# A first norm summed from rows of x, the norm of group A in other steps, and products of the identity beside the transposes

## The chip, the cores and the metric

The kernel runs on one core of one Trainium2 chip, as one launch. The time is the device time in microseconds (us). Matrix products run on TensorE (PE), whose operands come from SBUF and whose sums go to PSUM; VectorE (DVE), ScalarE (ACT) and GpSimd (POOL) do the rest. SyncE (SP) and ACT issue the transfers from memory. The engines run side by side, each through its own queue in order, and wait for each other on semaphores.

## What is computed

Two transformer blocks over one sequence of 512 tokens of width 1024, in float32. The change touches the first block alone:

```python
h = rms_norm(x, norm_mix_pre)            # mean of x*x over the 1024 columns of a token
proj = h @ w_in                          # 1024 -> 1536
qa, ka, va, qb, kb, vb = split(proj)     # 8 heads of 64 and 2 key heads, twice
qa = rope(rms_norm(qa, q_norm_a)); ka = rope(rms_norm(ka, k_norm_a))
out_a = global_attention(qa, ka, va)
out_b = window_attention(rope(qb), rope(kb), vb, sink_b)
mixed = concat(rms_norm(out_a, group_norm_a), rms_norm(out_b, group_norm_b)) @ w_out
x = x + rms_norm(mixed, norm_mix_post)
# a gated feed-forward follows, and a second block with other mixers
```

## The kernel before

**Products.** Activations lie with features on the 128 partitions and the 512 tokens along the row. Each wide product is made as three: weight and activation are split into a high and a low part (`w_hi`, `w_lo`, `h_hi`, `h_lo`), and `three` (L492) sums hi*hi, hi*lo and lo*hi in one PSUM bank. Weights come in units of 1 MB in three slots: SP loads a unit to `w_raw` (`load`, L420), `split` makes the high part on ACT (L981) and the low part on DVE (L433). A chunk is 128 output columns: 8 input tiles, so 24 products of 128x512.

**Start.** `in1` is the product with w_in, in chunks j = 0 to 11; chunks 9 to 11 are made during attention. Chunks 0 and 1 are made together (`first_units`, L516), tile after tile, as the eight tiles of x and the four quarters of unit 0 land: ACT makes `h_hi` (L1030) and the quarters' high parts, DVE the low parts (L1514 to L1520). h leaves out the norm's factor, a number per token, which goes in later. Its sum of squares: ACT squares each tile of x, POOL adds them up in `sqsum` (L462), and PE sums `sqsum` and the last square over the partitions with `ones` (`total`, L547, eight products). Then DVE has the variance, ACT the first guess of the root (`guess`, L996), DVE refines it (`factors`, L1461), and PE turns it along the rows (`factor`, L589). `beside` (L662) places this small work on PE behind the chunks: `total` behind chunk 2, `factor` behind chunk 3; `item` (L600) transposes V or sums the squares of a normed head over its 64 rows; `spread_heads` (L575) turns the heads' factors. A chunk's bank is free once ACT has copied it (`evacuate`, L1090); the chunks rotate over three banks. `rope` (L1552) is the rotation on DVE, one chunk after the other; `finish_normed` in it waits for `spread_heads`. The tables and masks `c1` (1.25 MB) are loaded from ACT's queue behind the first tile; `p_t`, used in the second block, is loaded to `hf` and split (`p_hi`, `p_lo`) at the start too.

**Attention** is one loop over 64 steps s, a step being one query block of 128 for one head (`STEPS`, L92): 0 to 31 global, 32 to 63 window. On PE (L718 to L745): on even s the scores of the pair of steps s+2 and s+3, and one of four parts of the weighted sum of an earlier pair; then the transposes of step s; then the norms' small work. DVE (L1626): the reciprocal and the scaling of `prob` for step s, then the maximum for step s+2. ACT (L1140): the exponential of step s, then the copy of the transposed block s-2 out of PSUM, then small work. The wait in question, on PE:

```python
pe.wait_ge(pn_ready, s + 1)      # DVE has scaled prob of step s
if s >= 2:
    pe.wait_ge(pt_ready, s - 1)  # ACT has copied step s-2 out of PSUM
for kb in range(k0, k1):
    last = nc.tensor.transpose(...)
```

**The norm of group A**, over the four output tiles `OT[:, 0:4]` of the global heads, is laid in steps 43 to 57 by `NORM_A_STEP` = 43: ACT squares one tile in each of steps 43 to 46, into two tiles of `sq` in turn, and before the third and fourth waits for PE to have summed an earlier one (L988); PE sums them in steps 45 to 48 (`sum_part`, L558, four products each); variance in 49, guess in 50, root in 51, `factor` in 52, and in steps 53 to 57 DVE scales (L1473) and makes low parts (L1477), ACT the high parts in 54 to 57. Group B's follows from step 58 on and ends behind the loop. `out1`, the product with w_out, starts behind the last weighted sums, once DVE has split its two units (L1648, L1649) behind its own loop.

## Time and profile before

| | |
|---|---|
| median of 3 runs | 1349.41 us (1348.96 to 1351.08) |
| profiled execution | 1350.37 us, span 1348.3 us, 2.1 us around it |
| PE busy | 1323.9 us, 98% of the span |
| DVE, ACT, POOL busy | 662.4, 538.8, 103.8 us |
| granted TensorE clock, mean | 0.994 |
| start of the transposes of step 40 | 149.32 us |
| last transposes done, start of the last weighted sums | 190.02 us |

The profile shows when each engine ran what, what it waited for, and the clock that TensorE was granted, 1.00 being 2.4 GHz and 0.50 being 1.2 GHz. Busy times of PE overlap, since its products are pipelined: what a product costs in a row of products is the distance of the starts. A float32 product that isn't split by the kernel appears as two matmuls, so the eight products of `total` stand as x8 twice. A time given for a line of several instructions is their whole stretch.

### The profile page before, as it was taken

To read this page: it belongs to the slowest core of one execution; us is meant where nothing else is said; L and a number is where in the kernel's file an instruction comes from. 1 tells how busy PE (TensorE), PEld (TensorE's weight loads), DVE (VectorE), ACT (ScalarE), POOL (GpSimd) and SP (SyncE) were. 2 spreads that over 40 slices of the span, in tenths; PEclk is the share of its full clock that TensorE was granted. 3 is DMA by queue.
4 is the path that set the end of the run, shared out by engine and by line. 5 is a ranking of instruction groups with operands and counts; after the bars stand their busy time and mean duration, and the time that the engine had idled before them with its cause. 6 is when DMAs were issued, how large, how long until landed. Compare 5 with 4: busy or idle time off the path is not lost.

```text
span 1348.3 us, 14835 instructions
## 1 busy us (share of the span) xinstructions
PE 1323.9 (98%) x6172; PEld 1062.7 (79%) x6172; DVE 662.4 (49%) x906; ACT 538.8 (40%) x732; POOL 103.8 (8%) x103
## 2 busy tenths in 40 slices
PE   7999999999999999999999999999999999999997
PEld 5874558888888888887888888888888888888877
DVE  6787574663544432227434445563544444423246
ACT  6558665442322322224225555542423232322234
POOL 3000003400000000003000001012000000001012
PEclk9999899999999999999999999999999999999999
DMA  6110012033232222331322111233222222223321
GB/s 247 63 63 1 0 64 94 32 125 98 103 107 99 84 82 91 104 109 54 129 87 86 61 60 61 78 105 107 96 94 94 94 94 94 82 90 104 100 94 63
DMA packets 20594, 117.75 MB, mean 87 GB/s; under 512 B 2480, under 2 KB 2864, under 8 KB 9904
## 3 DMA queue, kind: packets, MB, share of 16 engines
q1 hardware_dynamic: 19680, 114.79, 25.0%
q10 hardware_dynamic: 848, 2.01, 0.4%
q8 instruction: 49, 0.80, 0.2%
q14 instruction: 17, 0.14, 0.0%
HBM read 114.70 MB, written 2.10 MB: 87 GB/s over the span
## 4 chain that ended last, share of the span: by engine, by line
PE 95%; DVE 2%; ACT 1%; DMA 1%; issue 0%; SPq 0%; DVEq 0%; ACTq 0%
PE ps L490 93%; PE ps L735 2%; DMA w_raw<-weights 1%; DVE h_lo L1428 0%; ACT prob L979 0%; DVE w_lo L1421 0%; DVE prob L1425 0%; DVE hf L1428 0%; PE ps L923 0%; ACT w_hi L979 0%; PE ps L585 0%; PE ps L573 0%; DVE OUT L1425 0%; DVE hf L1421 0%; ACT h_hi L979 0%
## 5 line engine op out<-in xcount | busy, mean ns | idle before, releaser
L490 PE MATMUL ps<-h_hi,w_hi 128*128 128x512 f32 (+1 forms) x1256 | 494.0, 393 | 11.8 <-DVE w_lo L1421 10.7
L490 PE MATMUL ps<-h_lo,w_hi 128*128 128x512 f32 (+1 forms) x1256 | 489.4, 390 | 0.0
L490 PE MATMUL ps<-h_hi,w_lo 128*128 128x512 f32 (+1 forms) x1256 | 489.3, 390 | 0.0
L1421 DVE TENSOR_TENSOR w_lo<-w_raw,w_hi 128x2048 fp32r<-128x2048 f32 (+2 forms) x117 | 242.0, 2072 | 271.8 <-ACT w_hi L979 271.6
L490 PEld LDWEIGHTS ps<-h_hi,w_hi 128*128 128x128 f32 x1256 | 237.1, 189 | 67.8 <-issue 14.6
L979 ACT ACTIVATE w_hi<-w_raw 128x2048 fp32r<-128x2048 f32 (+2 forms) x117 | 201.4, 1722 | 199.2 <-DMA w_raw<-weights 199.0
L490 PEld LDWEIGHTS ps<-h_hi,w_lo 128*128 128x128 f32 x1256 | 237.0, 189 | 49.5
L490 PEld LDWEIGHTS ps<-h_lo,w_hi 128*128 128x128 f32 x1256 | 236.9, 189 | 48.9 <-issue 1.0
L466 POOL TENSOR_TENSOR sqsum<-sqsum,sq 128x512 f32<-128x512 f32 x59 | 86.4, 1465 | 834.8 <-ACT sq L979 833.5
L490 PE MATMUL ps<-mid_hi,w_hi 128*128 128x512 f32 x352 | 136.9, 389 | 0.0
L490 PE MATMUL ps<-mid_lo,w_hi 128*128 128x512 f32 x352 | 136.9, 389 | 0.0
L490 PE MATMUL ps<-mid_hi,w_lo 128*128 128x512 f32 x352 | 136.9, 389 | 0.0
L1421 DVE TENSOR_TENSOR hf<-ps,factors_sb 128x512 f32<-128x512 f32 (+1 forms) x57 | 38.7, 681 | 191.8 <-PE ps L490 191.6
L979 ACT ACTIVATE mid_hi<-hf 128x512 fp32r<-128x512 f32 x44 | 27.8, 633 | 209.1 <-DVE hf L1421 209.1
L490 PEld LDWEIGHTS ps<-mid_lo,w_hi 128*128 128x128 f32 x352 | 66.1, 188 | 13.8
L490 PEld LDWEIGHTS ps<-mid_hi,w_hi 128*128 128x128 f32 x352 | 66.1, 188 | 13.7
L490 PEld LDWEIGHTS ps<-mid_hi,w_lo 128*128 128x128 f32 x352 | 66.1, 188 | 13.7
L979 ACT ACTIVATE sq<-sq 128x512 f32<-128x512 f32 x44 | 27.7, 632 | 88.7 <-DVE sq L1421 88.7
L979 ACT ACTIVATE h_hi<-X,gain 128x512 fp32r<-128x512 f32 x40 | 28.9, 722 | 58.1 <-DVE X L1421 55.7
L1621 DVE TENSOR_REDUCE nmax<-ps 128x1 f32<-128x512 f32 (+2 forms) x64 | 37.5, 587 | 14.5 <-PE ps L490 14.4
L735 PEld LDWEIGHTS ps<-ident,prob 128*128 128x128 f32 x208 | 22.6, 143 | 27.1 <-DVE prob L1425 13.4
L1421 DVE TENSOR_TENSOR sq<-ps,factors_sb 128x512 f32<-128x512 f32 x44 | 30.0, 687 | 23.4 <-PE ps L490 23.4
(184 smaller groups left out, 1095.9 us busy)
## 6 DMA issues: line engine op xcount, KB each, us to landing
w_raw<-weights SPq DMA_DIRECT2D x81, 1024.0 KB, 4.8
w_raw<-weights SPq DMA_DIRECT2D x32, 704.0 KB, 4.1
out<-OUT SPq DMA_DIRECT2D x8, 256.0 KB, 2.7
X<-x_t SPq DMA_DIRECT2D x3, 512.0 KB, 7.5
c<-constants ACTq DMA_DIRECT2D x1, 1280.0 KB, 9.5
w_raw<-weights SPq DMA_DIRECT2D x4, 256.0 KB, 8.4
wp_raw<-weights SPq DMA_DIRECT2D x1, 1024.0 KB, 7.0
X<-x_t SPq DMA_DIRECT2D x2, 256.0 KB, 4.0
```

The source lines that it names most:

```text
L466: nc.gpsimd.tensor_tensor(sqsum[:, :], sqsum[:, :], sq[:, j % 2, :], ALU.add).then_inc(nm.summed.sem, 1)
L490: return nc.tensor.matmul(out, lhsT, rhs, start=start, stop=stop, skip_group_check=loose)
L735: last = nc.tensor.transpose(ps[:, tr_bank(s), (kb - k0) * P:(kb - k0 + 1) * P], prob[:, s % 3, (kb - k0) * P:(kb - k0 + 1) * P], ident[:, :])
L979: return nc.scalar.activation(out, in_, func, **kw)
L1421: return nc.vector.tensor_tensor(out, a, b, op)
L1621: nc.vector.tensor_reduce(nmax[:, s:s + 1], ps[:, s % 4, at:end], AX.X, ALU.max, negate=True).then_inc(nmax_ready, 1)
```

## The change

It does six things.

- **The sum of squares of the first norm** is made from x itself, tokens on partitions: four transfers of 0.5 MB bring blocks of 128 tokens to the tile of `PT` (unused so far), ACT squares each block of 128x1024 in place and adds along the row with `accum_out` (`row_squares`), behind the copy of chunk 2. The eight squares on ACT, POOL's adds and PE's `total` go. DVE's part moves behind unit 2 (`first_factors`), and the turning half of `rope(1)` ahead of that.
- **Transfers**: `c1` moves from ACT's queue to SP's, behind unit 1; the rows of x come behind unit 2; `p_t` and its split move into chunks 2 to 6 of `in1`, the masks to chunk 6.
- **PE beside the chunks**: `factor` and each `spread_heads` come one chunk later or at the same one (`SPREAD_AFTER`).
- **14 products of zeros** of 128x128 (`WARM`) on PE before the first real product.
- **The norm of group A**: the squares in steps 18, 26, 34 and 42, into four tiles, so that none waits; the sums in 33, 35, 37 and 44; variance, guess, root and turning in 46 to 49; scaling, high and low parts one a step in 50 to 61. Group B squares into four tiles too.
- **The identity times itself**, a float32 product of 128x128, in each of the steps 40 to 63, to the bank of the transposes, between the wait for `pt_ready` and that for `pn_ready`, whose order is turned.

```diff
-NORM_A_STEP = 43
+SQUARES_A, SUMS_A = (18, 26, 34, 42), (33, 35, 37, 44)
+VAR_A, GUESS_A, ROOT_A, SPREAD_A = 46, 47, 48, 49
+SCALE_A, HIGH_A, LOW_A = (50, 53, 56, 59), (51, 54, 57, 60), (52, 55, 58, 61)
+WARM = 14
+KEPT_BUSY = range(40, 64)
 SQUARES_B = (60, 62)
...
+SPREAD_AFTER = {4: 0, 5: 1, 6: 2, 7: 3}
...
                 self.kind = kind
+                tiles = [sq[:, 0, :], sq[:, 1, :], hf[:, 0, :], hf[:, 1, :]]
+                self.squared = (tiles[2:] + tiles[:2] if kind == "split" and before.kind != "split" else tiles
+                                if kind == "split" else tiles[:2])
...
-            for u in range(1, U_OUT1 + SLOTS):
+            load(1)
+            sp.dma_start(c1[:, :], consts[:, C1_AT:]).then_inc(c1_landed, 16)
+            load(2)
+            for b in range(NB):
+                sp.dma_start(x_rows[:, b * D:(b + 1) * D], x[b * P:(b + 1) * P, :]).then_inc(rows_landed[b], 16)
+            for u in range(3, U_OUT1 + SLOTS):
                 load(u)
...
-            sum_squares(n_mix_pre)
...
+            zeros = prob[:, 0, 0:P]
+            pe.wait_ge(zeroed, 1)
+            for _ in range(WARM):
+                mm(ps[:, SIDE_BANK, 0:P], zeros, zeros)
             first_units("in1", 0, 1, KS, h_hi, h_lo, parts_of(n_mix_pre.lo))
 
             def beside(j):
 
-                if j == 2:
-                    total(n_mix_pre)
-                if j == 3:
+                if j == 4:
                     factor(n_mix_pre)
                 for i in (0, 1) if j == 2 else (j - 1,):
                     item(i)
-                if j >= 2 and ORDER1[j - 2] in NORMED:
-                    spread_heads(NORMED.index(ORDER1[j - 2]))
+                if j in SPREAD_AFTER:
+                    spread_heads(SPREAD_AFTER[j])
...
-                pe.wait_ge(pn_ready, s + 1)
                 if s >= 2:
                     pe.wait_ge(pt_ready, s - 1)
+                if s in KEPT_BUSY:
+                    mm(ps[:, tr_bank(s), 0:P], ident[:, :], ident[:, :])
+                pe.wait_ge(pn_ready, s + 1)
                 for kb in range(k0, k1):
                     last = nc.tensor.transpose(ps[:, tr_bank(s), (kb - k0) * P:(kb - k0 + 1) * P],
                                                prob[:, s % 3, (kb - k0) * P:(kb - k0 + 1) * P], ident[:, :])
                 last.then_inc(tr_done, 1)
-                if 2 <= s - NORM_A_STEP < 6:
-                    sum_part(n_group_a, s - NORM_A_STEP - 2)
-                if s == NORM_A_STEP + 9:
+                if s in SUMS_A:
+                    sum_part(n_group_a, SUMS_A.index(s))
+                if s == SPREAD_A:
                     factor(n_group_a)
                 if s in SQUARES_B:
...
             def square(nm, j, src):
-                if j >= 2:
-                    act.wait_ge(*nm.summed(j - 1 if nm.kind == "split" else j))
-                af(sq[:, j % 2, :], src, ACT.Square).then_inc(nm.squares.sem, 1)
+                if j >= len(nm.squared):
+                    act.wait_ge(*nm.summed(j))
+                af(nm.squared[j % len(nm.squared)], src, ACT.Square).then_inc(nm.squares.sem, 1)
...
-                if k == 0:
-                    act.dma_start(c1[:, :], consts[:, C1_AT:]).then_inc(c1_landed, 16)
-                else:
-                    square(n_mix_pre, k - 1, X[:, k - 1, :])
-            square(n_mix_pre, KD - 1, X[:, KD - 1, :])
-            act.dma_start(hf[:, :, :], pT.rearrange("(k p) s -> p k s", p=P)).then_inc(p_landed, 16)
             split(1)
-            act.wait_ge(p_landed, 16)
-            af(p_hi[:, :, :], hf[:, :, :], ACT.Copy).then_inc(p_hi_ready, 1)
...
+            def row_squares(b):
+
+                act.wait_ge(rows_landed[b], 16)
+                block = x_rows[:, b * D:(b + 1) * D]
+                row = af(block, block, ACT.Square, accum_out=stat[:, 4, b:b + 1])
+                if b == NB - 1:
+                    row.then_inc(n_mix_pre.total.sem, 1)
...
                 if j == 2:
+                    for b in range(NB):
+                        row_squares(b)
                     guess(n_mix_pre)
+                    act.dma_start(hf[:, :, :], pT.rearrange("(k p) s -> p k s", p=P)).then_inc(p_landed, 16)
                     finish(0)
                     finish(1)
                 if 3 <= j:
                     finish(j - 1)
                 if 4 <= j:
                     swap_keys(j - 3)
+                if j == 5:
+                    act.wait_ge(p_landed, 16)
+                    af(p_hi[:, :, :], hf[:, :, :], ACT.Copy).then_inc(p_hi_ready, 1)
+                if j == 6:
+                    act.wait_ge(c0_landed, 32)
+                    act.wait_ge(c1_landed, 16)
+                    af(ident_r[:, :], ident[:, :], ACT.Copy).then_inc(masks_ready, 1)
+                    af(mask_r[:, :, :], c1[:, C_MASK - C1_AT:C_MASK - C1_AT + 2 * P].rearrange("p (m c) -> p m c", m=2),
+                       ACT.Copy).then_inc(masks_ready, 1)
...
-                if NORM_A_STEP <= s < NORM_A_STEP + 4:
-                    square_group(n_group_a, 0, s - NORM_A_STEP)
-                if s == NORM_A_STEP + 7:
+                if s in SQUARES_A:
+                    square_group(n_group_a, 0, SQUARES_A.index(s))
+                if s == GUESS_A:
                     guess(n_group_a)
-                if NORM_A_STEP + 11 <= s < NORM_A_STEP + 15:
-                    high_one(n_group_a, h_hi, s - (NORM_A_STEP + 11), 0)
+                if s in HIGH_A:
+                    high_one(n_group_a, h_hi, HIGH_A.index(s), 0)
...
+            act.wait_ge(*n_group_a.lo(4))
...
+            def apply_scale(nm, src, name, k):
+
+                if k == 0:
+                    dve.wait_ge(*nm.factor(1))
+                if k >= 2:
+                    dve.wait_ge(*nm.lo(k - 1))
+                stt(hf[:, k % 2, :], src[:, k, :], gcol(name, k), ps[:, nm.r_bank, :], ALU.mult, ALU.mult
+                    ).then_inc(nm.f32.sem, 1)
+
+            def apply_low(nm, dst_hi, dst_lo, k, n0):
+
+                dve.wait_ge(*nm.hi(k + 1))
+                low(dst_lo[:, n0 + k, :], hf[:, k % 2, :], dst_hi[:, n0 + k, :]).then_inc(nm.lo.sem, 1)
...
+            nc.vector.memset(prob[:, 0, 0:P], 0.0).then_inc(zeroed, 1)
...
-            dve.wait_ge(p_hi_ready, 1)
-            low(p_lo[:, :, :], hf[:, :, :], p_hi[:, :, :]).then_inc(p_lo_ready, 1)
-            split(2)
-            dve.wait_ge(c0_landed, 32)
-            variance(n_mix_pre)
-            dve.wait_ge(*n_mix_pre.var(1))
-            for n in range(2):
-                ts(eps_columns[:, n:8:2], stat[:, 0, :], EPS, ALU.mult)
-            factors(n_mix_pre)
-            dve.wait_ge(c1_landed, 16)
...
+            def turned_halves(j, scale, scale_rot, cos, sin):
+
+                dve.wait_ge(evac_act, EVAC["in1", j][1])
+                m = mark(swapped(rt[:, 1, :], y_of(j)))
+                stt(rt[:, 0, :], y_of(j), scale, c1[:, cos:cos + S], ALU.mult, ALU.mult)
+                dve.wait_ge(dve_self, m)
+                link(stt(rt[:, 1, :], rt[:, 1, :], scale_rot, c1[:, sin:sin + S], ALU.mult, ALU.mult))
+
+            def first_factors():
+
+                dve.wait_ge(*n_mix_pre.total(1))
+                ts(stat[:, 0, :], stat[:, 4, :], 1.0 / D, ALU.mult, EPS, ALU.add).then_inc(n_mix_pre.var.sem, 1)
+                dve.wait_ge(*n_mix_pre.var(1))
+                for n in range(2):
+                    ts(eps_columns[:, n:8:2], stat[:, 0, :], EPS, ALU.mult)
+                factors(n_mix_pre)
...
+                if ahead:
+                    turned_halves(j, scale, scale_rot, cos, sin)
+                    return
...
+                if j > 1:
+                    turned_halves(j, scale, scale_rot, cos, sin)
...
+            dve.wait_ge(c1_landed, 16)
+            rope(1, ahead=True)
+            split(2)
+            first_factors()
             for j in range(1, LATE1 - 1):
                 rope(j)
                 if j % 2 == 0:
                     split(j // 2 + 2)
                 if j == 2:
                     scale_tables()
+                if j == 6:
+                    dve.wait_ge(p_hi_ready, 1)
+                    low(p_lo[:, :, :], hf[:, :, :], p_hi[:, :, :]).then_inc(p_lo_ready, 1)
...
-                if s == NORM_A_STEP + 6:
+                if s == VAR_A:
                     variance(n_group_a, 4 * P)
-                if s == NORM_A_STEP + 8:
+                if s == ROOT_A:
                     factors(n_group_a)
-                if NORM_A_STEP + 10 <= s < NORM_A_STEP + 15:
-                    apply_one(n_group_a, OT[:, 0:4, :], "group_norm_a", h_hi, h_lo, s - (NORM_A_STEP + 10), 0)
+                if s in SCALE_A:
+                    apply_scale(n_group_a, OT[:, 0:4, :], "group_norm_a", SCALE_A.index(s))
+                if s in LOW_A:
+                    apply_low(n_group_a, h_hi, h_lo, LOW_A.index(s), 0)
```

## Rows read from the trace of the kernel before

**Rows 1.** The page's chain that ended last, its shares by engine.

```profile
PE 95%; DVE 2%; ACT 1%; DMA 1%; issue 0%; SPq 0%; DVEq 0%; ACTq 0%
```

**Rows 2.** Stretches: length; busy us and count by engine; PEclk; DMA share; GB/s.

```profile
34.50:37.60 3.10, 3.10 (x9) 2.36 (x8) 2.21 (x6) 2.81 (x5) 0.00 (x0) 0.50 0.00 0
...
141.34:149.32 7.98, 7.98 (x48) 3.99 (x46) 5.73 (x25) 5.47 (x18) 0.00 (x0) 1.00 0.00 0
...
155.00:161.30 6.30, 4.27 (x31) 3.12 (x31) 1.79 (x9) 3.20 (x10) 0.00 (x0) 0.93 0.00 0
161.30:166.80 5.50, 5.45 (x21) 3.39 (x21) 1.77 (x8) 1.21 (x6) 0.00 (x0) 0.50 0.00 0
```

**Rows 3.** PE at the start, in order of time: start, stretch, what, [idle before].

```profile
7.08 0.77 PE L490 MATMUL ps<-h_hi,w_hi 128*128 128x512 f32 x1 [7.08 <-DVE w_lo L1421]
...
8.92 0.63 PE L490 MATMUL ps<-h_lo,w_hi 128*128 128x512 f32 x1
...
20.29 0.57 PE L490 MATMUL ps<-h_hi,w_hi 128*128 128x512 f32 x1 [1.81 <-DVE w_lo L1421]
...
24.71 0.39 PE L490 MATMUL ps<-h_hi,w_hi 128*128 128x512 f32 x1
```

**Rows 4.** ACT and DVE at the start, in order of time.

```profile
13.72 0.63 ACT L979 ACTIVATE w_hi<-w_raw 128x512 fp32r<-128x512 f32 x1 [1.38 <-DMA w_raw<-weights]
...
15.51 2.96 DVE L1428 SCALAR_TENSOR_TENSOR h_lo<-X,gain,h_hi 128x512 fp32r<-128x512 f32 x2 [0.44 <-ACT h_hi L979]
...
20.17 1.90 ACT L979 ACTIVATE w_hi<-w_raw 128x2048 fp32r<-128x2048 f32 x1
...
22.09 2.29 DVE L1421 TENSOR_TENSOR w_lo<-w_raw,w_hi 128x2048 fp32r<-128x2048 f32 x1 [0.26 <-ACT w_hi L979]
...
23.52 1.06 ACT L979 ACTIVATE p_hi<-hf 128x1024 fp32r<-128x1024 f32 x1 [1.46 <-DMA hf<-p_t]
```

**Rows 5.** Stretches as in rows 2, and ACT's transfer queue (q10) from 10 to 12 us.

```profile
0.00:10.00 10.00, 2.92 (x7) 2.37 (x8) 3.36 (x4) 5.16 (x8) 2.05 (x6) 1.00 0.81 260
10.00:15.00 5.00, 4.32 (x18) 3.15 (x17) 4.29 (x4) 3.62 (x8) 2.90 (x3) 1.00 1.02 418
...
q10 hardware_dynamic: 68, 0.70, 81.8%
```

**Rows 6.** PE around chunk 3 of in1, in order of time.

```profile
30.16 0.95 PE L490 MATMUL ps<-ones,sqsum 128*128 128x1 f32 x8
...
31.86 0.64 PE L605 MATMUL ps<-ident,PP 128*128 128x128 f32 x4
...
33.15 0.48 PE L490 MATMUL ps<-h_hi,w_hi 128*128 128x512 f32 x1
...
40.31 0.60 PE L573 MATMUL ps<-ident,stat 128*128 128x128 f32 x4
```

**Rows 7.** DVE in in1: the step of the rotation that waits for chunk 3.

```profile
41.73 0.17 DVE L1428 SCALAR_TENSOR_TENSOR rt<-ps,rt 128x8 f32<-128x8 f32 x1 [4.89 <-PE ps L490]
```

**Rows 8.** Attention from step 40: PE's first and last rows, an ACT row, a row of waits.

```profile
149.32 0.68 PE L735 MATMUL ps<-ident,prob 128*128 128x128 f32 x4
...
159.57 0.63 ACT L979 ACTIVATE sq<-OT 128x512 f32<-128x512 f32 x1 [1.65 <-PE ps L490]
...
190.02 0.65 PE L490 MATMUL ps<-PT,VB 128*64 128x256 f32 x4
...
PE ps L735 <- DVE prob L1425: 5.2, 5, 1.9
```

**Rows 9.** A float32 product of 128x512 between products of the usual kind.

```profile
266.43 1.02 PE L490 MATMUL ps<-sqsum,ones 128*128 128x512 f32 x2
...
267.52 0.40 PE L490 MATMUL ps<-h_lo,w_hi 128*128 128x512 f32 x1
```

**Rows 10.** DVE's norm work in step 55, from the chain in order of time.

```profile
175.31 0.66 DVE hf L1428
175.97 0.60 DVE h_lo L1421
```

More of the change, by code:

```diff
@@ L94, with build @@
     (1, 2 * c + n, b, max(b - 1, 0), min(b + 2, NB)) for c in range(NH // 2) for b in range(NB) for n in range(2)]
-def build(nc, xT, pT, weights, gains, consts, out):
+def build(nc, xT, x, pT, weights, gains, consts, out):
     import concourse.bass as bass
@@ L236, in build @@
         x_landed = [sem(f"x_landed{i}") for i in range(5)]
+        rows_landed = [sem(f"rows_landed{b}") for b in range(NB)]
         gain_landed, c0_landed, c1_landed, c2_landed, p_landed = (
@@ L302, in __init__ @@
                 for e in NORM_EVENTS:
-                    norm_counts[e] += (n if e == "squares" else self.sums if e == "summed" else
+                    norm_counts[e] += (0 if kind == "late" and e in ("squares", "summed") else n if e == "squares" else self.sums if e == "summed" else
                                        n_f32 if e == "f32" else
@@ L547, in total @@
             def total(nm):
-                if nm.before is None:
-                    pe.wait_ge(c0_landed, 32)
                 for src, ready, n in ((sqsum[:, :], nm.summed, nm.n), (sq[:, (nm.n - 1) % 2, :], nm.squares, nm.n)):
@@ L561, in sum_part @@
                 for b in range(NB):
-                    last = mm(ps[:, nm.ss_bank, b:b + 1], sq[:, j % 2, b * P:(b + 1) * P], ones[:, 0:1],
+                    last = mm(ps[:, nm.ss_bank, b:b + 1], nm.squared[j][:, b * P:(b + 1) * P], ones[:, 0:1],
                               j == 0 and b == 0, True, loose=True)
@@ L602, in item @@
                 if c in V1:
+                    if j == 0:
+                        pe.wait_ge(c0_landed, 32)
                     pe.wait_ge(evac_act, EVAC["in1", j][1])
```

32 lines of the change are left out of this document (8 added, 24 removed).

## The prediction

> **What bounds the kernel now.** The chain of work that ended last comes first: PE carries 95% of it, DVE 2% and transfers 1% [rows 1]. So a microsecond is won only where PE stands still, runs at the lower clock, or does work that can go. The stretches with their granted clock and PE's order of time show where that is within the reach of the change. From 7.08 to 24.71 us PE makes the 48 products of the first two chunks [rows 3]; later ones lie 0.227 us apart (24 from 24.71 to 30.16 [rows 3, 6]), so 48 need 10.9 us, and they took 17.6. Behind chunk 2 the eight small products of `total` take 1.70 us, 30.16 to 31.86, and chunk 3 takes 7.16 us (33.15 to 40.31) instead of 5.45 [rows 6]: for 3.1 us of it the clock is 0.50 [rows 2]. In attention, from the transposes of step 40 at 149.32 to 190.02, 40.70 us, PE waits five times for `prob`, 5.2 us in all [rows 8], and for 5.5 us the clock is 0.50 [rows 2]. The rest of the trace, from out1 on, the change leaves as it is, and I carry it over.
>
> **The start.** What holds PE in the first 17.6 us is read from ACT, DVE and the transfers. ACT waits 1.38 us for a quarter of the weights, which lands at 13.7 [rows 4], though it is the seventh piece of SP's queue, which holds 2.25 MB up to and with it. The transfers had moved 2.6 MB by 10 us and go at 0.42 MB per us from then on [rows 5], 4.15 MB by 13.7; in 10 to 12 us, 0.70 MB of it were ACT's queue, that is c1 [rows 5]. With c1 behind unit 1 on SP's queue, that share goes to x and the weights. Taking off the 0.17 MB of gains and constants and the 1.25 of c1, SP's queue had moved some 2.7 MB when its first 2.25 had landed, so I add 0.5 MB to each piece. Then, with M for the queue's bytes up to a piece, it lands at 10 + (M + 0.5 + 0.17 - 2.6) / 0.42: the last quarter (M = 3.0) at 12.5 us, unit 1 (4.0) at 14.9, c1 (5.25) at 17.9, unit 2 (6.25) at 20.3, the last rows of x (8.25) at 25.0. Also gone are ACT's eight squares and POOL's adds; DVE's two `h_lo` at 15.51 took 2.96 us [rows 4], 1.48 each, while the adds ran. I take 0.65 for each, near to what the same kind of instruction takes in rows 10 without them. PE, starting at 7.1, is then held by its own 10.9 us and some 0.4 of waiting for the second quarter: done at 18.4. Unit 1 needs 1.9 on ACT and 2.3 on DVE behind its landing [rows 4]: 14.9 + 1.9 + 2.3 = 19.1. This is later, so chunk 2 begins at 19.1 instead of 24.71: **5.6 us won**. Ends: 6.3 (PE alone decides, 18.4) and 4.5 (each piece lands 1.1 us later, as the skew of 0.5 MB doubled would do).
>
> The 14 products of zeros are meant for the first products, which run at the low rate (0.63 us long at 8.92 against 0.39 at 24.71 [rows 3]). A float32 product of 128x512 costs 1.09 - 0.23 = 0.86 us between others (266.43 to 267.52, less one product of the usual kind [rows 9]), so one of 128 columns 0.21, or 0.43 at half the clock; 14 of them take 3 to 6 us. They start behind a memset at about 1 us and end before 7.08, when PE had nothing else: no cost. If they bring the clock up before 7.08, unit 0 ends at 18.4, otherwise about a microsecond later, at 19.4; since unit 1 is ready at 19.1 anyhow, they are worth 0.3 us, which is in the 5.6. Cost the other way: at half the clock throughout they end at 7.0, just in time.
>
> Moving c1 is where a rule speaks against the change. The Trainium skill (DMA: Bandwidth & Descriptors, Issuing engines are not separate DMA queues) says that transfers issued on several engines run on the same 16 DMA engines and interleave, and that issuing on several only saves issue time. Read so, c1's place would matter little, and the quarters would land as before. That is the second rival below; the row of 10 to 12 us, with four fifths of the bytes on ACT's queue, speaks for the order in the queue mattering, and I go by it.
>
> **Chunks 2 to 8.** `total` goes from PE: **1.7 us won**, with nothing to hide it before, since PE was dense there. The half clock in chunk 3 came behind 3.0 us of nothing but small products and transposes, 30.16 to 33.15 [rows 6]. What is left in their place is `item(0)` and `item(1)`, 1.3 us (31.86 to 33.15); behind chunk 3, 40.31 to 41.95 in the trace, a stretch of 1.6 us of the same kind brought no half clock. So I take the drop as gone: **1.7 us won**, ends 0 and 1.7.
>
> What was moved must keep up with chunks that begin 5.6 us earlier and lack 3.4 us in between. ACT copies chunk 2 by 25.6, then squares four blocks. One activation of 128x1024 took 1.06 [rows 4]; with the read of the sum 1.1 each, so the sum is there at 30.0, the root at 31.5. `factor` stands behind chunk 4, at about 37.7 in the new time, 6 us later: covered. The first `spread_heads` needs ACT's widening, which stands behind the copy of V and the high part of unit 3 (1.9): about 36.5, against 38.1: 1.6 us of slack. Chunk 6 needs the low part of unit 3, which DVE makes behind `rope(2)`. That waits for the turned factors of chunk 1: at 38.6, then 1.8 us of small work, 2.3 of split, so 42.7; chunk 6 begins at about 45.3: 2.6 us of slack. DVE then runs about 2 us closer to PE than before, when it had idled 4.89 us [rows 7]; its later waits cover that, and p_lo (a 128x1024 instruction of some 1.2 us) falls into its wait for chunk 8. So all this costs nothing; if the sum came more than 1.6 us late, each further microsecond would cost one. The 2 MB of rows delay only unit 3, which lands by 27.5 and is wanted at 34.
>
> **Attention.** Within steps 40 to 63 the trace has 40.70 us, less 5.2 of waits, less half of the 5.5 at half clock (2.75): 32.75 us of PE work. The sums of group A in steps 33, 35 and 37 are merely moved on PE, in front of step 40, at the same price, for PE is dense there as well (7.98 of 7.98 in 141.34 to 149.32 [rows 2]). 24 products of the identity add 24 x 0.21 = 5.0 us where PE doesn't wait: 37.8. Where PE waits for `prob` they cost nothing, since they stand in front of that wait. The three waits around 155 to 161 come from ACT's squares, which stood behind PE's sums (1.65 us of idle at 159.57 [rows 8]); with four tiles they go, and so does the half clock behind them. The two around 176 and 181 come from DVE, whose scaling and low part, 1.26 us, fell on each of the steps 53 to 57 [rows 10]. Spread over steps 50 to 61, DVE has 12 x 0.955 (5.73 us in six steps [rows 2]) + 4 x 1.26 = 16.5 us; PE in 12 steps has about 14.4 plus 2.5 of identities, 16.9. The two are nearly even, so neither hides the other wholly: I put 1.3 us of waits on it, a quarter of those of now. That makes 39.1: **1.5 us won** (40.7 - 39.1, rounded down). Ends: -1 (every product on the path and 3 us of the waits left, and a little) and +4 (most of the products in waits).
>
> Behind the loop nothing changes: DVE splits out1's two units behind its step 63, PE has the last weighted sums beside that, and the new wait of ACT for group A's last low part (step 61) is met before.
>
> **The sum.** 5.6 + 1.7 + 1.7 + 1.5 = 10.5 us. Against the profiled execution that is 1350.4 - 10.5 = 1339.9, with a span of 1337.8; that execution lies 1.0 us above the median of the runs, from which I count: 1349.4 - 10.5 = 1338.9, say 1339.0.
>
> **The rivals.**
> - *The transfers don't follow the queue's order* or the skew is larger: the quarters land as before, from 13.7 on, and only POOL's and ACT's work is saved. DVE's split of unit 1 ended at 24.4 [rows 4]; without the 1.5 us or so that POOL's adds cost the last low parts in front of it, chunk 2 begins at about 22.9, 1.8 us won instead of 5.6: 1342.8. For it: the skew is already 0.5 MB. Chance 0.12.
> - *The products don't do what they say*: the half clock in attention stays (2.75 us), or comes elsewhere, and the zeros leave the start cold. 1338.9 + 2.75 + 0.3 = 1342.0. For it: in chunk 3 the clock fell though PE hadn't been idle before. Chance 0.15.
> - *The identities fall into waits* more than I think, because the loop through DVE and ACT, not PE, sets the step once PE has no clock loss; attention then wins 4 to 5: 1335.8. Chance 0.13.
> - *Slower*: the first norm's sum comes late, because the rows of x are last in SP's queue and ACT has the squares in front of the copies of the chunks. PE would wait in `factor` and `spread_heads` one for one beyond 1.6 us of slack. To eat up 10.5 us the sum would have to be there after 30.0 + 1.6 + 10.5 = 42.1, so the rows would land 12 us late, at 37: 15 us later and it is 1352. The rates of rows 5 speak against it. Chance 0.03.
>
> **How the numbers follow.** The forecast, 1339.0, has the remaining 0.57, between 1336 and 1342. The ends of the terms give 1349.4 - (6.3 + 1.7 + 1.7 + 4) = 1335.7 and 1349.4 - (4.5 + 1.7 + 0 - 1) = 1344.2; with the rivals in it, the range is 1334.8 to 1344.0. A difference of 0.2% (2.7 us) is about what a measurement of this kernel can tell from none: faster than 1346.7 in 0.94, within in 0.03, slower than 1352.1 in 0.03.
>
> **What would show it.** Right: chunk 2 begins near 19 us and no row of the start shows half clock behind 7.1; the first `h_lo` take below 0.8; chunks 2 to 8 lie 5.5 us apart at clock 1.00, with `factor` behind chunk 4 and no wait before it; step 40 begins near 140.3 + 2.4 of moved sums = 142.7; the identities run at 0.21 from start to start, no stretch of attention has clock 0.50, and DVE is busy evenly over steps 50 to 61. Wrong: PE waiting for `w_lo` of unit 0 beyond 13 us (transfers), for `rt` behind chunk 4 (late sum), or for `prob` more than 2 us in all beside the identities (their price is then not the matter, the loop is).

## The result, and the profile after

| | before | after |
|---|---|---|
| median of the runs | 1349.18 us (1348.35 to 1351.08, 4 runs) | 1342.08 us (1341.92 to 1342.24, 4 runs) |
| profiled execution, span | 1350.37, 1348.3 us | 1342.09, 1340.1 us |
| chunk 2 begins | 24.71 us | 19.41 us |
| chunk 3 ends | 40.31 us | 31.86 us |
| transposes of step 0 | 81.33 us | 73.39 us |
| PE's work of step 40 behind the weighted sums (transposes; in the changed kernel an identity first, its transposes at 145.63) | 149.32 us | 145.31 us |
| last weighted sums | 190.02 us | 181.91 us |
| out1 starts | 192.96 us | 184.85 us |

By the medians it is faster by 7.1 us (a quotient of 0.9947), where 10.5 were forecast. The ratio on record, which isn't the quotient of these medians, is 0.9938 (95% interval 0.9925 to 0.9952); the interval holds both and lies clear of 1. The time lies inside the range, 3.1 us above the predicted number. From out1 on nothing moved: it starts 8.1 us earlier and the span is 8.2 us shorter. PE still carries the chain that ended last:

```profile
PE 94%; DVE 3%; ACT 1%; DMA 1%; issue 0%; SPq 0%; DVEq 0%; ACTq 0%
```

PE of the changed kernel in order of time (start, stretch, what, [idle before]) answers [rows 3] and [rows 6]:

```profile
1.12 5.23 PE L505 MATMUL ps<-prob 128*128 128x128 f32 x28 [1.12 <-DVE prob L1543]
7.29 0.47 PE L505 MATMUL ps<-h_hi,w_hi 128*128 128x512 f32 x1 [0.94 <-DVE w_lo L1447]
7.60 0.40 PE L505 MATMUL ps<-h_lo,w_hi 128*128 128x512 f32 x1
...
19.41 0.50 PE L505 MATMUL ps<-h_hi,w_hi 128*128 128x512 f32 x1 [0.60 <-DVE w_lo L1447]
...
31.86 1.05 PE L505 MATMUL ps<-c,ysq 128*128 128x2 f32 x8
...
38.33 0.60 PE L586 MATMUL ps<-ident,stat 128*128 128x128 f32 x4
...
58.60 0.66 PE L598 MATMUL ps<-ident,rt 128*128 128x128 f32 x4 [0.24 <-ACT rt L998]
```

The zeros fill 1.12 to 6.35 us, and the second real product follows the first by 0.31 us and the next ones by 0.23. Chunk 2 begins 5.3 us earlier, chunk 3 ends 8.45 us earlier, and `factor` (L586) has no wait before it. ACT and DVE of the same stretch, which answer [rows 4]:

```profile
10.14 1.46 DVE L1454 SCALAR_TENSOR_TENSOR h_lo<-X,gain,h_hi 128x512 fp32r<-128x512 f32 x2
...
12.67 0.64 ACT L998 ACTIVATE w_hi<-w_raw 128x512 fp32r<-128x512 f32 x1
...
15.12 1.92 ACT L998 ACTIVATE w_hi<-w_raw 128x2048 fp32r<-128x2048 f32 x1 [1.20 <-DMA w_raw<-weights]
...
17.07 2.29 DVE L1447 TENSOR_TENSOR w_lo<-w_raw,w_hi 128x2048 fp32r<-128x2048 f32 x1 [2.27 <-ACT w_hi L998]
```

Stretches of the changed kernel (length; busy us and count on PE, PEld, DVE, ACT, POOL; granted clock, DMA share, GB/s), to be held against [rows 2]. None of the stretches of 5 us has a clock below 1.00 before the last 10 us of the span. For the first products this view isn't enough, since it gives 1.00 where they lie 0.43 us apart too (5 to 10 us of the kernel before); there the distance of the starts counts:

```profile
30.00:35.00 5.00, 5.00 (x27) 4.08 (x26) 3.10 (x15) 4.02 (x11) 0.00 (x0) 1.00 0.62 185
...
160.00:165.00 5.00, 4.86 (x34) 2.78 (x30) 4.00 (x13) 3.05 (x10) 0.00 (x0) 1.00 0.01 3
165.00:170.00 5.00, 4.83 (x33) 2.95 (x33) 4.39 (x17) 3.47 (x11) 0.00 (x0) 1.00 0.00 0
```

Attention in order of time on PE, which answers [rows 8], and then, from the view of waits of 130 to 190 us, PE's waits for `prob` (us in total, times, longest):

```profile
99.18 1.17 PE L754 MATMUL ps<-ident,prob 128*128 128x128 f32 x8
...
102.35 1.17 PE L754 MATMUL ps<-ident,prob 128*128 128x128 f32 x8
...
108.68 1.39 PE L754 MATMUL ps<-ident,prob 128*128 128x128 f32 x8
...
123.19 0.63 PE L754 MATMUL ps<-ident,prob 128*128 128x128 f32 x4 [0.61 <-DVE prob L1451]
...
145.31 0.49 PE L505 MATMUL ps<-ident 128*128 128x128 f32 x2
145.63 0.38 PE L754 MATMUL ps<-ident,prob 128*128 128x128 f32 x2
145.85 0.39 PE L505 MATMUL ps<-ident 128*128 128x128 f32 x2
146.08 0.38 PE L754 MATMUL ps<-ident,prob 128*128 128x128 f32 x2
...
181.91 0.65 PE L505 MATMUL ps<-PT,VB 128*64 128x256 f32 x4
```

```profile
PE ps L754 <- DVE prob L1451: 0.8, 3, 0.4
```

The waits for `prob` fell from 5.2 us to 0.8 us. Four rows tell of losses: a wait of 0.24 us at 58.60, one of 0.61 us at 123.19, eight transposes that take 1.17 us where before they took 1.10, and the eight of steps 18 and 19, which take 1.39:

```profile
107.08 1.10 PE L735 MATMUL ps<-ident,prob 128*128 128x128 f32 x8
```

That last row is the kernel before's, in the same view.

### The profile page after: what moved, and what is told of

Read it like the earlier page. It is cut to its first block, busy times and chain, and to the rows that moved or that the text cites. A ratio compares the mean times of both kernels' runs of the same rounds, so it can differ in the third digit from the quotient of the medians.

```text
span 1340.1 us, 14918 instructions
## 1 busy us (share of the span) xinstructions
PE 1326.2 (99%) x6232; PEld 1067.0 (80%) x6232; DVE 656.6 (49%) x907; ACT 538.1 (40%) x732; POOL 93.2 (7%) x95
## 4 chain that ended last, share of the span: by engine, by line
PE 94%; DVE 3%; ACT 1%; DMA 1%; issue 0%; SPq 0%; DVEq 0%; ACTq 0%
PE ps L505 92%; PE ps L754 2%; DMA w_raw<-weights 1%; DVE w_lo L1447 1%; ACT w_hi L998 0%; DVE rt L1454 0%; PE ps L942 0%; DVE nmax L1665 0%; DVE prob L1451 0%; ACT hf L998 0%; SPq L444 0%; SPq L440 0%; PE ps L586 0%; DVE OUT L1451 0%; DVE hf L1447 0%
## 5 line engine op out<-in xcount | busy, mean ns | idle before, releaser
L998 ACT ACTIVATE w_hi<-w_raw 128x2048 fp32r<-128x2048 f32 (+2 forms) x117 | 201.2, 1722 | 199.7 <-DMA w_raw<-weights 199.5
L482 POOL TENSOR_TENSOR sqsum<-sqsum,sq 128x512 f32<-128x512 f32 x52 | 76.4, 1469 | 825.2 <-ACT sq L998 824.5
L998 ACT ACTIVATE mid_hi<-hf 128x512 fp32r<-128x512 f32 x44 | 27.8, 633 | 209.1 <-DVE hf L1447 209.1
L998 ACT ACTIVATE sq<-sq 128x512 f32<-128x512 f32 x44 | 27.7, 632 | 89.8 <-DVE sq L1447 89.8
L998 ACT ACTIVATE h_hi<-X,gain 128x512 fp32r<-128x512 f32 x40 | 28.9, 723 | 58.5 <-DVE X L1447 55.4
L998 ACT ACTIVATE prob<-ps,nmax 128x512 f32<-128x512 f32 (+2 forms) x64 | 39.1, 610 | 5.7 <-DVE nmax L1665 5.5
```

Of the source, the lines that this page charges most:

```text
L482: nc.gpsimd.tensor_tensor(sqsum[:, :], sqsum[:, :], sq[:, j % 2, :], ALU.add).then_inc(nm.summed.sem, 1)
L998: return nc.scalar.activation(out, in_, func, **kw)
```

## The experiments

Eleven kernels, run in three batches with the kernel before beside each: the kernels without identities, without zeros, with the old order of waits in steps 0 to 39 and with the square in step 30 (before: 1350.06 us, 9 runs); the identity twice, the two with the old norm and c1 back (1349.18 us, 24 runs); the combined one, the masks later and c1 alone (1350.06 us, 17 runs). Ratios are to the runs of the kernel before in the same batch.

Medians that lie less than 2 us apart need care, because some executions lose time at the very end, where no edit reaches. From the start of out1 to the end of the span it is 1155.3 us in the kernel before and the changed one, but 1157.0 in the profiled execution of the kernel with the square in step 30, whose clock fell there:

```profile
1330.00:1335.00 5.00, 3.92 (x23) 3.68 (x22) 2.53 (x11) 2.07 (x7) 0.00 (x0) 0.71 0.00 0
```

So the starts of steps and of out1 in the traces are the surer measure of a small cost.

### Attention: the identities, the order of the waits, the squares

**Without the identities.**

```diff
-KEPT_BUSY = range(40, 64)
+KEPT_BUSY = ()
```

> The changed kernel without the 24 products of the identity; all else as in it. Theory A (they hold the clock): the products cost PE 24 x 0.22 = 5.3 us in a row, of which some 1.5 fall into waits; without them the clock falls to 0.50 for 5 us or more somewhere in steps 40 to 63, which gives 2.5 us or more back, and the waits for prob grow: between 1339.5 and 1343, with a stretch of clock 0.50. Rival B (the schedule of the norm alone removed the half clock, since the wait in front of it is gone): no stretch at 0.50, and the attention is 3.5 to 5 us shorter: 1337 to 1338.5.

Measured: 1341.01 us (1340.55 to 1341.18, 5 runs), ratio 0.9934 (0.9922 to 0.9947). A stretch of it, its waits for `prob` and the start of out1:

```profile
160.00:165.00 5.00, 3.53 (x26) 2.19 (x24) 4.52 (x16) 3.58 (x10) 0.00 (x0) 1.00 0.02 5
```

```profile
PE ps L754 <- DVE prob L1451: 4.2, 7, 1.0
```

```profile
183.40 0.50 PE L505 MATMUL ps<-h_hi,w_hi 128*128 128x512 f32 x1
```

The waits are back (4.2 us), PE is busy for 3.53 of 5 us, and the clock stays at 1.00 all the same. Out1 starts 1.45 us earlier than in the changed kernel, of which 0.12 us lies ahead of step 40. So the identities cost 1.1 us by the medians (1342.08 - 1341.01), 1.3 by the profiles, and in this trace of the new schedule they guard against nothing. Rival B's mechanism holds, a schedule that keeps the clock by itself; its price doesn't: it put attention 3.5 to 5 us shorter and the time at 1337 to 1338.5, and the gain is 1.3 us, since 4.2 us of waits come back. The time alone, which lies in theory A's range, would have spoken for the wrong one.

**The identity twice.**

```diff
                 if s in KEPT_BUSY:
                     mm(ps[:, tr_bank(s), 0:P], ident[:, :], ident[:, :])
+                    mm(ps[:, tr_bank(s), 0:P], ident[:, :], ident[:, :])
```

> The changed kernel with the product of the identity twice in each of the steps 40 to 63 instead of once. The look at the kernel without it gave 1341.0 against 1342.1, so the first one costs 1.1 us net although PE spends 24 x 0.22 = 5.3 us on it. Theory (it falls into waits for prob, which are nearly used up by it): the second finds about 1 us of waits left, so it costs 4 us or more, 1346 to 1347.4. Rival (the price of one is well under 0.22 us in the pipeline, and what is hidden is not a wait): the second costs what the first did, 1343.2.

Measured: 1345.64 us (1345.28 to 1347.02, 10 runs), ratio 0.9974 (0.9964 to 0.9984). PE at step 40:

```profile
145.44 0.71 PE L505 MATMUL ps<-ident 128*128 128x128 f32 x4
145.99 0.38 PE L755 MATMUL ps<-ident,prob 128*128 128x128 f32 x2
```

Two take 0.55 us from start to start where one took 0.32 (145.31 to 145.63): 0.23 us for the second, 5.5 us in 24 steps. Out1 starts at 188.41, 3.6 us later. The first identity took 5.3 us of PE (24 x 0.22) or more and moved the time by 1.1, the second moved it by 3.6: the first was mostly paid from waits, and it used them up, as the theory had it, though the time lies 0.4 us below the theory's range (1346 to 1347.4). The rival's 1343.2 is further off.

**The old norm of group A, with the identities and without.** Its sums, scaling and low parts go back to their old steps, with two tiles for the squares and the wait in front of the third and fourth; the second kernel also has `KEPT_BUSY = ()`. The turned order of the two waits stays in both.

```diff
-SQUARES_A, SUMS_A = (18, 26, 34, 42), (33, 35, 37, 44)
-VAR_A, GUESS_A, ROOT_A, SPREAD_A = 46, 47, 48, 49
-SCALE_A, HIGH_A, LOW_A = (50, 53, 56, 59), (51, 54, 57, 60), (52, 55, 58, 61)
+SQUARES_A, SUMS_A = (43, 44, 45, 46), (45, 46, 47, 48)
+VAR_A, GUESS_A, ROOT_A, SPREAD_A = 49, 50, 51, 52
+SCALE_A, HIGH_A, LOW_A = (53, 54, 55, 56), (54, 55, 56, 57), (54, 55, 56, 57)
...
-                if j >= len(nm.squared):
-                    act.wait_ge(*nm.summed(j))
+                if j >= 2:
+                    act.wait_ge(*nm.summed(j - 1 if nm.kind == "split" else j))
```

> The changed kernel with the norm of group A (and the two tiles of squares, with ACT's wait for PE's sums) as before, in steps 43 to 57; the identities stay. Theory: the waits around steps 46 and 47 and around 55 to 57 come back, 3 to 5 us of them, of which the identities fill some 1.2; the clock stays at 1.00 in attention, because PE has a product in each step: 1343 to 1345. Rival: the clock falls to 0.50 behind the long wait all the same, and 2.75 us more are lost: 1346 to 1348.

> As the run before it in this list, but without the identities, so that attention is that of the kernel before behind the new start. Theory (the wait in front of it makes the clock fall): a stretch of 5 us at 0.50 as in the trace of before, and steps 40 to the last weighted sums take 40.7 us: 1342.1 + 4.1 - 2.4 of sums in front = 1343.8 if the waits are alike, 1344 to 1345 in all. Rival (the half clock there was a matter of the hour of the clock's window and not of the schedule): no stretch at 0.50, 1341 to 1342.

Measured: with the identities 1347.85 us (1346.38 to 1350.48, 10 runs), ratio 0.999 (0.9978 to 1.0002); without 1343.88 us (1341.99 to 1347.83, 5 runs), ratio 0.9958 (0.9937 to 0.998). With the identities, a PE row and three stretches:

```profile
155.32 0.49 PE L504 MATMUL ps<-ident 128*128 128x128 f32 x2 [1.61 <-ACT PT L997]
```

```profile
155.00:160.00 5.00, 4.68 (x22) 2.77 (x22) 2.07 (x11) 1.74 (x7) 0.00 (x0) 0.65 0.00 0
160.00:165.00 5.00, 5.00 (x22) 4.42 (x22) 1.47 (x6) 2.77 (x9) 0.00 (x0) 0.50 0.01 3
165.00:170.00 5.00, 5.00 (x30) 2.41 (x27) 3.17 (x15) 2.33 (x7) 0.00 (x0) 0.82 0.01 3
```

Without them, the waits and two stretches:

```profile
PE ps L753 <- DVE prob L1449: 5.6, 5, 2.0
```

```profile
155.00:160.00 5.00, 5.00 (x23) 3.05 (x23) 1.51 (x5) 1.56 (x5) 0.00 (x0) 0.57 0.00 0
160.00:165.00 5.00, 5.00 (x17) 2.51 (x18) 2.81 (x14) 1.92 (x7) 0.00 (x0) 0.50 0.01 2
```

The clock falls in both, in the profiled executions, which lie 2.5 and 2.3 us above their medians. It doesn't fall for as long in every one: two of the five runs without the identities (1341.99 and 1342.19 us) had a mean clock of 0.997 against the profiled one's 0.993. The row shows why an identity doesn't bridge the wait: PE now stands still ahead of the identity (1.61 us, `<-ACT PT`), since it is the wait for the copy of `PT` that comes last once ACT is held by its square, and the product is placed behind that wait. ACT waits 3.8 us in two times for PE's sums there. So with the identities the rival held, and without them the theory (1343.8, or 1344 to 1345, and a stretch at 0.50). It is the schedule that keeps the clock, and not the product, which costs 4.0 us beside the old schedule by the medians (a rough number, since the runs without it spread by 5.8) and 3.0 by the start of out1 in the two traces (191.89 against 188.88).

**The old order of the two waits in steps 0 to 39.**

```diff
+                if s not in KEPT_BUSY:
+                    pe.wait_ge(pn_ready, s + 1)
                 if s >= 2:
                     pe.wait_ge(pt_ready, s - 1)
                 if s in KEPT_BUSY:
                     mm(ps[:, tr_bank(s), 0:P], ident[:, :], ident[:, :])
-                pe.wait_ge(pn_ready, s + 1)
+                    pe.wait_ge(pn_ready, s + 1)
```

> The changed kernel with the two waits in front of the transposes in their old order in steps 0 to 39 (pn_ready first, then pt_ready); the identity's steps as they are. Theory: with the order turned, four pairs of steps take 3.17 us each where they took 3.10 before; 20 pairs of such steps cost 0.065 us each, so 1.0 to 1.3 us come back: 1340.8 to 1341.1, and the eight transposes take 1.10 us again instead of 1.17. Rival: the pace of a pair is set by ACT, which has the squares of group A now, and nothing changes: 1342.1, pairs at 3.17.

Measured: 1341.68 us (1341.33 to 1342.74, 5 runs), ratio 0.9942 (0.993 to 0.9955). PE:

```profile
105.42 1.10 PE L756 MATMUL ps<-ident,prob 128*128 128x128 f32 x8
```

The 1.10 us are back, and a pair of steps takes 3.10 us (102.32 to 105.42) instead of 3.17 (99.18 to 102.35). From step 0 to step 40 it is 71.35 us (73.52 to 144.87) instead of 71.92: 0.57 us for the order of two waits that are both met. That is about half of what was expected, because only nine of the 20 pairs ahead of step 40 are slower in the turned order, by 0.05 to 0.07 us each; those of steps 2 to 9, for one, keep the same distance in both. Why the order costs anything the trace doesn't say.

**The second square in step 30.**

```diff
-SQUARES_A, SUMS_A = (18, 26, 34, 42), (33, 35, 37, 44)
+SQUARES_A, SUMS_A = (18, 30, 34, 42), (33, 35, 37, 44)
```

> The changed kernel with the second square of group A in step 30 instead of 26. Steps 25 to 28 also hold the four copies of the second V on ACT. Theory: ACT is full from 118.9 to 125.6 us there, so the square's 0.52 us is passed on to PE, which stands 0.61 us before step 27: in step 30 it is hidden, 1341.5. Rival: steps 28 to 31 are as full on ACT and the wait only moves: 1342.1.

Measured: 1341.7 us (1341.4 to 1343.06, 5 runs), ratio 0.9941 (0.9928 to 0.9955). The profiled execution took 1343.06 us, with the fall of the clock at the end that is shown above; up to out1 (184.18 against 184.85) it is ahead of the changed kernel. PE at steps 26 and 27, in one group now:

```profile
121.77 1.39 PE L754 MATMUL ps<-ident,prob 128*128 128x128 f32 x8
```

No wait is left between the two, and step 0 to step 40 takes 71.40 us (73.25 to 144.65), 0.52 less. In steps 25 to 28 ACT also copies V, one block a step, and in the changed kernel the square stands between such a copy and the exponential that DVE's `prob` waits for:

```profile
120.75 0.39 ACT L998 ACTIVATE VB<-ps,stat 128x128 f32<-128x128 f32 x1
121.00 0.66 ACT L998 ACTIVATE hf<-OT 128x512 f32<-128x512 f32 x1
121.52 0.71 ACT L998 ACTIVATE prob<-ps,nmax 128x512 f32<-128x512 f32 x1
```

### The start

**Without the zeros.**

```diff
-WARM = 14
+WARM = 0
```

> The changed kernel without the 14 products of zeros. Theory (from the trace of the changed kernel): the first 7 or so real products run 0.43 us apart instead of 0.227, so unit 0 ends about 1.0 to 1.4 us later, at 19.7 to 20.1 instead of 18.7, while unit 1 is ready at 19.35 anyhow: chunk 2 begins 0.3 to 0.7 us later, 1342.4 to 1342.8. Rival: the clock comes up and falls again at another place of the start, as it did before at 20.3 us, and the loss is 2 us or more.

Measured: 1342.85 us (1342.67 to 1343.89, 5 runs), ratio 0.995 (0.9937 to 0.9962). PE:

```profile
7.25 0.77 PE L505 MATMUL ps<-h_hi,w_hi 128*128 128x512 f32 x1 [7.25 <-DVE w_lo L1447]
7.81 0.63 PE L505 MATMUL ps<-h_lo,w_hi 128*128 128x512 f32 x1
```

The first products are 0.43 us apart again, up to 11.64 us, and step 0 begins at 74.05 instead of 73.39. The zeros are worth 0.7 us, as expected (0.3 to 0.7).

**c1 back on ACT's queue**, in the changed kernel.

```diff
             load(1)
-            sp.dma_start(c1[:, :], consts[:, C1_AT:]).then_inc(c1_landed, 16)
             load(2)
...
+                if k == 0:
+                    act.dma_start(c1[:, :], consts[:, C1_AT:]).then_inc(c1_landed, 16)
```

> The changed kernel with the tables and masks (c1, 1.25 MB) loaded from ACT's queue behind the first tile, as before; all else as in it. Theory (the order in the queue decides): the third and fourth quarter of unit 0 land 3 us later, at 13.7 and 15.5 us or so, PE stands for them, unit 1 is split at about 22, and chunk 2 begins at 21.5 to 22.5 instead of 19.41: 1344.1 to 1345.1. Rival (POOL's adds and the squares on ACT held the start, and c1's place matters little): chunk 2 begins before 20, 1342.1 to 1342.6.

Measured: 1345.58 us (1345.0 to 1346.74, 8 runs), ratio 0.9973 (0.9963 to 0.9983). ACT and PE:

```profile
13.61 0.63 ACT L997 ACTIVATE w_hi<-w_raw 128x512 fp32r<-128x512 f32 x1 [2.93 <-DMA w_raw<-weights]
...
17.99 1.92 ACT L997 ACTIVATE w_hi<-w_raw 128x2048 fp32r<-128x2048 f32 x1 [1.17 <-DMA w_raw<-weights]
...
22.29 0.50 PE L504 MATMUL ps<-h_hi,w_hi 128*128 128x512 f32 x1 [1.46 <-DVE w_lo L1448]
```

Unit 1 lands 2.9 us later (17.99 against 15.12), chunk 2 begins 2.9 us later. The theory holds in the trace, and the time lies 0.5 us above its range (1344.1 to 1345.1): the 1.25 MB of c1 in the other queue delay what the start waits for by about their own length (1.25 / 0.42 = 3.0 us at the rate of [rows 5]).

**c1 alone moved**, in the kernel before.

```diff
-            for u in range(1, U_OUT1 + SLOTS):
+            load(1)
+            sp.dma_start(c1[:, :], consts[:, C1_AT:]).then_inc(c1_landed, 16)
+            for u in range(2, U_OUT1 + SLOTS):
                 load(u)
...
-                if k == 0:
-                    act.dma_start(c1[:, :], consts[:, C1_AT:]).then_inc(c1_landed, 16)
-                else:
+                if k:
                     square(n_mix_pre, k - 1, X[:, k - 1, :])
```

> The kernel before with one edit: c1 goes from ScalarE's queue to SyncE's, behind unit 1. The first norm's squares, the adds on GpSimd and the eight products behind chunk 2 stay. Theory (the queue's order is worth most of the gain of the start): the quarters of the weights land about 1 us earlier, unit 1 as in the changed kernel; the low parts stay slow at 1.48 each beside the adds, so chunk 2 begins near 21 instead of 24.7 and the time is 1345.2 to 1346.2. Rival (c1's place was worth something only because the squares and adds were gone as well): chunk 2 begins at 22.9 or later, 1347.4 or more. The half clock in chunk 3 stays by both.

Measured: 1350.09 us (1346.7 to 1352.18, 12 runs), ratio 0.9993 (0.9982 to 1.0004). My theory fell here, the rival held. As both had it, the half clock in chunk 3 stays (0.85 and 0.81 in the two stretches of 5 us from 30 to 40), and in this kernel `total` is still there; with c1 on ACT's queue and `total` gone no such stretch is below 1.00. POOL, DVE, ACT and PE:

```profile
10.93 9.74 POOL L468 TENSOR_TENSOR sqsum<-sqsum,sq 128x512 f32<-128x512 f32 x6 [1.74 <-ACT sq L981]
...
16.08 3.46 DVE L1428 SCALAR_TENSOR_TENSOR h_lo<-X,gain,h_hi 128x512 fp32r<-128x512 f32 x2
19.47 1.75 DVE L1421 TENSOR_TENSOR w_lo<-w_raw,w_hi 128x512 fp32r<-128x512 f32 x1
...
19.56 1.89 ACT L981 ACTIVATE w_hi<-w_raw 128x2048 fp32r<-128x2048 f32 x1
...
24.21 0.43 PE L492 MATMUL ps<-h_hi,w_hi 128*128 128x512 f32 x1
```

The data is there earlier, and nothing comes of it. POOL now adds without a pause, 1.62 us each, and beside it DVE's `h_lo` take 1.73 each and a `w_lo` of 128x512 takes 1.75; in the changed kernel, without the adds, they take 0.73 and 0.68. ACT's squares wait for POOL, and the high part of unit 1 stands behind them. A rule of the Trainium skill (SBUF — State Buffer, SBUF: two separate sides) says that an instruction of VectorE with two operands from SBUF and one of GpSimd share a pair of ports that is locked for a whole instruction, so that one stands while the other runs; the rows agree in that each slows the other down and both go at nearly one pace, 1.62 and 1.73 us an instruction. They don't show turns for the whole of every instruction: one of each alone would be 0.73 and 1.32 (the median of the 59 adds of the kernel before), 2.05 us a round, more than was measured. The start has two limits, then, the transfers and POOL's adds:

| chunk 2 begins | squares and adds stay | gone, zeros added, `p_t` later |
|---|---|---|
| c1 on ACT's queue | 24.71 | 22.29 |
| c1 on SP's queue | 24.21 | 19.41 |

The right column brings 2.4 us alone, c1's move 0.5, the two together 5.3. How the 2.4 divide between the adds, the squares, the zeros and the later `p_t` wasn't tried.

### The parts that pay, together

**No identities, the old order of the waits, the square in step 30**: the edits of three kernels above in one, with the old order now in every step.

> The changed kernel with three edits together: no identities, the two waits ahead of the transposes in the old order in every step, and the second square of group A in step 30 instead of 26. Theory (the three costs lie in different steps and add up): 1341.0 without the identities, less 0.55 for the waits' order in steps 0 to 39 and a little for steps 40 to 63, less 0.5 for the square: 1339.7 to 1340.1; step 40 begins at 144.1 to 144.4, and no wait stands before the transposes of step 27. Rival (the gains overlap, the loop through VectorE and ScalarE sets the pace once the TensorE work in it is shorter): 1340.5 or more, step 40 begins at 144.6 or later.

Measured: 1339.4 us (1339.21 to 1341.92, 6 runs), ratio 0.992 (0.9906 to 0.9934); the profiled execution took 1339.31. PE:

```profile
144.44 0.68 PE L751 MATMUL ps<-ident,prob 128*128 128x128 f32 x4
...
182.21 0.50 PE L504 MATMUL ps<-h_hi,w_hi 128*128 128x512 f32 x1
```

From step 0 (73.59) to step 40 it is 70.85 us, 1.07 less than in the changed kernel: 0.57 and 0.52 add up. Out1 starts 2.6 us earlier. Step 40 is 0.04 us later than the theory's bound, the time 0.3 us below it; the rival's overlap didn't show. It is 2.7 us below the changed kernel, and nothing here is faster by more than the runs tell.

**ACT's mask copies behind chunk 7 as well**, instead of chunk 6.

```diff
-                if j == 6:
+                if j == 7:
                     act.wait_ge(c0_landed, 32)
```

> As the last kernel, and ScalarE's two mask copies behind the copy of chunk 7 instead of chunk 6. Theory (the copies, 0.5 us, stood ahead of the widening for the fourth spread of the heads, on which TensorE waited 0.24 us at 58.60): that wait goes, the transposes of step 0 begin 0.2 to 0.3 us earlier than in the last kernel, and the time is about 0.2 us less, which the time alone can't tell. Rival (chunk 8 waits for something else next, the split or VectorE): the transposes of step 0 begin at the same time, and the wait is at another row.

Measured: 1339.78 us (1338.97 to 1341.77, 5 runs), ratio 0.9916 (0.9903 to 0.993). PE behind chunk 7:

```profile
58.64 0.66 PE L597 MATMUL ps<-ident,rt 128*128 128x128 f32 x4
```

The wait is gone, as the theory had it, and step 0 begins at 73.40 instead of 73.59. The rival has a part in it all the same: the row still stands 5.74 us behind the first product of its chunk, 5.57 at the other chunks, and ACT's widening in front of it (57.95) now waits 0.18 us for DVE. In the time the 0.2 us can't be told.

## Why the prediction was right or wrong

The time fell inside the range, and the four terms of the sum were right within 0.3 us. The step that failed is one that the sum holds at nothing: that what was moved costs nothing in `in1` and is merely moved, "at the same price", in steps 0 to 39. It cost 0.5 and 1.5 us. The range had a slip too: its bounds, 1334.8 and 1344.0, aren't the 1335.7 and 1344.2 to which the ends of the terms add up. Against the profiled execution the forecast was 1339.9 us; it took 1342.09, 2.2 us more. Another 0.9 us of the 3.1 come from the step from that execution to the median: before's lies 1.0 to 1.2 us above its median, after's on it.

- **The start**, 5.6 us: 5.3 measured (24.71 to 19.41). The landing of unit 1 was worked out as 14.9 and ACT took it up at 15.12, and the ends of 1.92 and 2.29 us behind it were right. The four rows of x came in time for ACT's squares at 26.20, and its sum of squares was there at 30.5, against 30.0.
- **`total` and chunk 3**, 1.7 + 1.7: 8.45 - 5.3 = 3.15 measured. No half clock came.
- **The rest of in1**, "all this costs nothing": 8.45 us ahead at the end of chunk 3, 7.94 at step 0, so 0.5 lost. 0.24 of it is the wait at 58.60. I had counted DVE's slack there, and the squares on ACT; what I left out were the masks, which the change moved ahead of ACT's 1.91 us of unit 5 (L998, `w_hi`) and of the widening (`rt`) that PE wants:

```profile
55.61 0.31 ACT L998 ACTIVATE ident_r<-ident 128x128 fp32r<-128x128 f32 x1
...
56.13 1.91 ACT L998 ACTIVATE w_hi<-w_raw 128x2048 fp32r<-128x2048 f32 x1
57.94 0.61 ACT L998 ACTIVATE rt<-rt 128x512 f32<-128x512 f32 x1
```

The wait puts the row 5.95 us behind the chunk's first product, 5.57 at the other chunks, which is 0.38 of the 0.5; 0.1 more is the first small row behind chunk 3, 0.91 us from start to start (31.86 to 32.77) where the others of its kind take 0.81.
- **Steps 0 to 39**, moved "at the same price": this is the largest miss. Before, step 40 stood 67.99 us behind step 0, after 71.92: 3.93 more, of which the three moved sums are 2.45 (0.82 each). The other 1.5 us I hadn't priced at all: 0.57 for the turned waits, which the change makes in all 64 steps and which I gave no price (in steps 40 to 63 I counted the identity alone); 0.52 for the square in step 26, where ACT was full; 0.4 is left, in the combined kernel too (70.85 - 67.99 - 2.45). The traces place it: steps 18 and 19 take 3.37 us from transposes to transposes there and 3.11 before, 0.26 for the square in step 18 (with no square in that step, in the kernels with the old norm, 3.17, which is the turned order's), and the three pairs with the moved sums are longer than before by 0.90, 0.82 and 0.89 us, 0.16 more than 2.45. The forecast of step 40, 142.7, was 2.6 us too early: 0.3 from the start, 0.25 from chunk 3, 0.5 and 1.5 from these two. It is this step that put the forecast 2 us off.
- **Attention from step 40**: 36.60 us to the last weighted sums, 40.70 before. Net of the moved sums that is 1.65 won, 1.5 forecast. The waits left are 0.8, not 1.3, and an identity is 0.22 us, or 0.32 at the first of a pair, not 0.21. The size was right; the reason was right only in part. The schedule alone brings it, as the kernels without the identities (1341.01) and with the old norm and without them (1343.88) show, and the identities take 1.1 of it back. That the term came out within 0.2 us is in part luck: by the two distances the identities took 24 x 0.27 = 6.5 us of PE and not 5.0, the waits 0.5 less than forecast, and the 1.0 us between isn't placed.
- **The zeros**, 0.3: 0.7 measured. Without them unit 0's end does count, since the wait ahead of chunk 2 is 0.60 us only.
- **The rivals.** That the transfers don't follow the order is out: chunk 2 began at 19.41, not at 22.9. Its 1342.8 lies closer to the time than the forecast does, by chance. That c1's place matters is what the kernel with c1 back shows, 2.9 us, and the rule of the Trainium skill (DMA: Bandwidth & Descriptors, Issuing engines are not separate DMA queues) that I weighed against the change agrees with the shared bytes but not with the reading that the place is then nearly free. That the products do nothing: half right. The identities don't keep the clock, but there was no drop left to keep it from, and the zeros did work. Its 1342.0 is the number nearest to the time, 0.1 us off, and that is luck too: none of the 3.05 us of which it is made was lost. That the identities fall into waits, with 4 to 5 us won in attention: no, 1.65 were won; but without them DVE does keep PE waiting for 4.2 us, which is the limit that this rival named. That late sums make it slower: no wait stood in `factor`.

## What to carry over

Before a change is costed at nothing, list what each engine does at the spot to which a thing is moved, for every thing that is moved there: here a mask copy of 0.5 us and a square of 0.66 us each stood in front of what PE wanted next. Price a product that keeps an engine busy against the waits it fills, and test the schedule without it first; once the long waits are scheduled away, it is pure cost. And where a start is held by transfers and by engines at once, try the parts singly: neither side of the table gave half of what both did.

## What was not expected of the hardware

- **The spread of a kernel's runs went with its waits.** The three experiments with the old norm of group A spread by 4.1, 5.8 and 5.5 us (10, 5 and 12 runs), the kernel before by 4.2, 7.8 and 5.4 (9, 24 and 17 runs); all those with the new schedule by 2.8 us or less. The time went with the mean granted clock: of the 24 runs the one of 1346.25 us had 0.997 and that of 1354.05 had 0.992; the kernel with the old norm alone had 0.997 at 1341.99 and 0.992 at 1347.83. The half clock, then, doesn't take the same length each time. Where in an execution it lay is known only of the profiled ones; there it lay behind waits in attention and behind one of 1.81 us at 20.29 in the kernel before, after which the products lie 0.43 us apart (one of 1.79 us at 21.37, with c1 moved alone, was followed by products 0.23 apart), behind the small products of chunk 3, and in some in the last 20 us, at a cost of up to 1.7 us.
- **Two waits that are both met cost up to 0.07 us a pair of steps more in one order than in the other** (1.17 against 1.10 us for eight transposes), in nine of 20 pairs.
- **DVE beside POOL's adds**: 1.73 us for what takes 0.73 alone; an add went from 1.32 to 1.62.
